# Attention over paged values: probabilities and values as unsplit fp32 in two column halves of TensorE, in place of a high and a low part on the whole array

## The reference, cut to what matters

```python
def mla_attend(q_lat, q_rope, ckv, krope, mask):
    s = (jnp.einsum('bthr,bsr->bhts', q_lat, ckv)
         + jnp.einsum('bthe,bse->bhts', q_rope, krope)).astype(jnp.float32)
    s = jnp.where(mask[None, None], s, -jnp.inf)
    p = jax.nn.softmax(s, axis=-1).astype(ckv.dtype)
    return jnp.einsum('bhts,bsr->bthr', p, ckv)
```

## Time and profile before

| | |
|---|---|
| time, median of 3 runs | 899.58 us (899.31 to 901.48) |
| the profiled execution, its own time | 901.31 us |
| its span in the profile | 899.5 us |
| granted TensorE clock in it | 0.998 |
| TensorE busy | 886.8 us, 99% |
| VectorE busy | 588.7 us, 65% |
| ScalarE busy | 472.5 us, 53% |

### The profile page before, as it was taken

How to read it: one execution, slowest core, us unless ns; L and a number is a source line. 1 busy time by engine, 2 the same in 40 slices (tenths; PEclk the granted TensorE clock), 3 DMA queues, 4 the chain that set the end, 5 groups by cost and what they waited for, 6 DMA issues and landing times. The chain is left out here.

```text
span 899.5 us, 15487 instructions
## 1 busy us (share of the span) xinstructions
PE 886.8 (99%) x5569; PEld 807.1 (90%) x5569; DVE 588.7 (65%) x984; ACT 472.5 (53%) x776; POOL 78.3 (9%) x79
## 2 busy tenths in 40 slices
PE   8999999999999999999999999999999999999996
PEld 8989999999999999999999999888887788888885
DVE  6535635442267678787878866867657697564767
ACT  6564431121233567657666753577755545353446
POOL 0003002413100000000000000000000011111022
PEclk9999999999999999999999999999999999999999
DMA  9694444232293577877787764332037546997586
GB/s 349 242 331 169 164 144 152 71 113 87 75 353 96 170 239 243 259 241 248 234 249 240 247 239 167 128 113 75 18 146 276 117 134 158 231 248 234 128 155 211
DMA packets 77164, 168.55 MB, mean 187 GB/s; under 512 B 9672, under 2 KB 44041, under 8 KB 75096
## 3 DMA queue, kind: packets, MB, share of 16 engines
q1 hardware_dynamic: 70960, 143.27, 47.1%
q0 software_dynamic: 4608, 16.78, 10.1%
q10 hardware_dynamic: 1520, 7.51, 2.3%
HBM read 156.14 MB, written 11.50 MB: 186 GB/s over the span
## 5 line engine op out<-in xcount | busy, mean ns | idle before, releaser
L67 PE MATMUL z<-x_hi,w_hi 128*128 128x288 f32 x512 | 152.6, 298 | 0.0
L69 PE MATMUL z<-x_hi,w_lo 128*128 128x288 f32 x512 | 150.8, 295 | 0.0
L68 PE MATMUL z<-x_lo,w_hi 128*128 128x288 f32 x512 | 150.8, 294 | 0.0
L184 ACT ACTIVATE w_hi<-w_raw 128x1024 fp32r<-128x1024 f32 (+2 forms) x62 | 64.9, 1046 | 134.7 <-PE z L69 52.5
L191 DVE TENSOR_TENSOR w_lo<-w_raw,w_hi 128x1024 fp32r<-128x1024 f32 (+2 forms) x62 | 77.2, 1247 | 69.8 <-ACT w_hi L184 69.3
L67 PEld LDWEIGHTS z<-x_hi,w_hi 128*128 128x128 f32 x512 | 96.1, 188 | 2.3 <-issue 0.2
L68 PEld LDWEIGHTS z<-x_lo,w_hi 128*128 128x128 f32 x512 | 96.1, 188 | 1.7 <-issue 0.2
L69 PEld LDWEIGHTS z<-x_hi,w_lo 128*128 128x128 f32 x512 | 96.0, 188 | 0.0
L1988 ACT ACTIVATE o_hi<-o_raw 128x1024 fp32r<-128x1024 f32 x50 | 52.9, 1060 | 78.0 <-PE pa_s L2901 33.3
L2214 DVE TENSOR_TENSOR o_lo<-o_raw,o_hi 128x1024 fp32r<-128x1024 f32 x50 | 61.1, 1222 | 42.6 <-ACT o_hi L1988 42.5
L69 PE MATMUL z_acc<-x_hi,w_lo 128*128 128x288 f32 x256 | 75.1, 293 | 0.0
(11 more groups left out here) (529 smaller groups left out, 2425.8 us busy)
## 6 DMA issues: line engine op xcount, KB each, us to landing
w_raw<-in_w_feat SPq DMA_DIRECT2D x56, 512.0 KB, 4.0
k_raw<-in_cache SPq DMA_DIRECT2D x128, 192.0 KB, 3.0
v_raw<-in_cache SPq DMA_DIRECT2D x128, 128.0 KB, 2.6
o_raw<-in_w_out POOLq DMA_DIRECT2D x30, 512.0 KB, 8.3
o_raw<-in_w_out SPq DMA_DIRECT2D x20, 512.0 KB, 8.5
w_raw<-in_w_mem_kv SPq DMA_DIRECT2D x16, 512.0 KB, 3.5
gate_spill<-gate_tmp SPq DMA_DIRECT2D x16, 288.0 KB, 3.2
mix<-gate_spill SPq DMA_DIRECT2D x4, 1152.0 KB, 11.1
```

What stands on the lines that cost most here:

```text
L67: pe.matmul(out, a[0], b[0], start=start, stop=False, skip_group_check=onto)
L68: pe.matmul(out, a[0], b[1], start=False, stop=False, skip_group_check=onto)
L69: return pe.matmul(out, a[1], b[0], start=False, stop=stop, skip_group_check=onto)
L184: act.activation(hi_slot(s, u)[:, lo:w], s.wraw[:, u % RAW, lo:w], ACT.Copy).then_inc(s.w_hi, 1)
```

## The change

The values are used where the DMA put them, in `v_raw`, and the probabilities are copied once, in fp32, to a `probs_t` of half the width. The 64 columns of a page's probabilities are the weights, so only half the columns of the array are used by a matmul. Its output goes to partitions 0 to 63 of `ps_o` for an even page of the quad and to 64 to 127 for an odd one. The copies of the values' high parts on ScalarE and of the low parts on VectorE are gone, and so are the low parts of the probabilities on VectorE. The two halves of `ps_o` are added as before, by the same instructions.

```diff
         vraw = at("v_raw", [P, VRING, 4, KVR])
-        vh = at("v_hi", [P, HRING, 4, KVR], F32R)
+        at.at += HRING * 4 * 4 * KVR
...
-        pt = at("probs_t", [P, NPAGE + 1, 2 * NS], F32R)
+        pt = at("probs_t", [P, NPAGE + 1, NS])
+        at.at += 4 * (NPAGE + 1) * NS
...
-                        act.activation(pt[:, 0:8, 0:NS], p_p[:].rearrange("p (g r) -> p g r", g=8), ACT.Copy).then_inc(pt_hi, 1)
+                        act.activation(pt[:, 0:8, :], p_p[:].rearrange("p (g r) -> p g r", g=8), ACT.Copy).then_inc(pt_hi, 1)
...
-                    m = n - VLAG + 1
-                    if 0 <= m < QUADS:
-                        values_hi(m)
...
-                def values_lo(m):
-                    dve.wait_ge(v_hi, m + 1)
-                    dve.tensor_tensor(vlo[:, m % VRING, :, :], vraw[:, m % VRING, :, :], f32(vh[:, m % HRING, :, :]),
-                                      ALU.subtract).then_inc(v_lo, 1)
...
-                        dve.tensor_tensor(pt[:, 0:8, NS:2 * NS], p_p[:].rearrange("p (g r) -> p g r", g=8),
-                                          f32(pt[:, 0:8, 0:NS]), ALU.subtract).then_inc(pt_lo, 1)
...
                         if m % 4 == 0:
-                            pe.wait_ge(pt_lo, 3 * (m // 4) + 1)
+                            pe.wait_ge(pt_hi, 3 * (m // 4) + 1)
                             if m:
                                 pe.wait_ge(o_sb, m // 4)
                         if m % 4 >= 2:
-                            pe.wait_ge(pt_lo, 3 * (m // 4) + m % 4)
-                        pe.wait_ge(v_lo, m + 1)
+                            pe.wait_ge(pt_hi, 3 * (m // 4) + m % 4)
+                        pe.wait_ge(v_in[m % VRING], 64 * (m // VRING + 1))
                         for j in range(4):
                             g = 4 * (m % 4) + j
-                            pe.matmul(p_o[:, 0:KVR], pt[:, g, :], vh[:, m % HRING, j, :], start=g == 0, stop=False)
-                            last = pe.matmul(p_o[:, 0:KVR], pt[:, g, :], vlo[:, m % VRING, j, :], start=False, stop=False)
+                            last = pe.matmul(p_o[mine(j, 0), 0:KVR], pt[:, g, :], vraw[:, m % VRING, j, :], start=g < 2, stop=False)
                         if m % 4 == 3:
-                            pe.wait_ge(zeros, 3)
-                            pe.matmul(p_o[:, 0:KVR], pt[:, 16, :], vs_hi[:], start=False, stop=False)
-                            last = pe.matmul(p_o[:, 0:KVR], pt[:, 16, :], vs_lo[:], start=False, stop=True)
+                            for i in range(2):
+                                c = slice(P * i, P * i + P)
+                                last = pe.matmul(p_o[mine(i, 0), c], pt[:, 16, :], vs[:, c], start=False, stop=True)
                         last.then_inc(pv, 1)
```

More of the change, by code:

```diff
@@ L808, in middle_stage @@
         ckt_s, krt_s = at("ckt_s", [P, 2 * NS]), at("krt_s", [P, NS])
-        vs_hi, vs_lo = at("vs_hi", [P, KVR], F32R), at("vs_lo", [P, KVR], F32R)
+        at.at += 2 * 4 * KVR
+        vs = s.kvn[:, 4, 0:KVR]
         pages = at("pages", [1, DB * NPAGE], I32)
@@ L828, in middle_stage @@
         klo = place(nc, kr_raw, "k_lo", [P, KRING, 4, KW], F32R)
-        vlo = place(nc, v_raw, "v_lo", [P, VRING, 4, KVR], F32R)
         at = Map(nc, kr_raw + 2 * 4 * 4 * KW)
@@ L868, in middle_stage @@
         rope_ps, roped, qrt_ps, qrt_hi, qrt_lo = sem("q_ropep"), sem("q_roped"), sem("q_qrtp"), sem("q_qrthi"), sem("q_qrtlo")
-        kt_ps, kt_sb, vs_done = sem("q_ktp"), sem("q_kts"), sem("q_vs")
+        kt_ps, kt_sb = sem("q_ktp"), sem("q_kts")
         s.middle_sums = z[:, (2 * FEATS - 1) % 3, 0:TH]
@@ L873, in middle_stage @@
         k_in, v_in = [sem(f"s_kin{i}") for i in range(KRING)], [sem(f"s_vin{i}") for i in range(VRING)]
-        kt_hi, kt_lo, kr_lo, v_hi, v_lo = sem("s_kthi"), sem("s_ktlo"), sem("s_krlo"), sem("s_vhi"), sem("s_vlo")
+        kt_hi, kt_lo, kr_lo = sem("s_kthi"), sem("s_ktlo"), sem("s_krlo")
         sc_ps, sc_low, sc_sb = sem("s_scps"), sem("s_sclow"), sem("s_scsb")
@@ L878, in middle_stage @@
         wqr_in, wqr_done = sem("o_wqrin"), sem("o_wqr")
-        pa_ps, pb_ps, pc_ps, pt_hi, pt_lo = sem("s_paps"), sem("s_pbps"), sem("s_pcps"), sem("s_pthi"), sem("s_ptlo")
+        pa_ps, pb_ps, pc_ps, pt_hi = sem("s_paps"), sem("s_pbps"), sem("s_pcps"), sem("s_pthi")
         pv, o_low, o_sb, ot_ps, ot_sb = sem("s_pv"), sem("s_olow"), sem("s_osb"), sem("s_otps"), sem("s_otsb")
@@ L981, in _ @@
                 pool.memset(krt_s[ROPE:P, :], 0.0).then_inc(zeros, 1)
-                pool.memset(f32(vs_hi[NS:P, :]), 0.0).then_inc(zeros, 1)
-                pool.memset(f32(vs_lo[NS:P, :]), 0.0).then_inc(zeros, 1)
-                pool.wait_ge(zeros, 3)
+                pool.wait_ge(zeros, 1)
                 pool.wait_ge(lat_ps, 1)
@@ L1016, in keys_hi @@
                     act.activation(kth[:, n % 2, :, :].rearrange("p c (j k) -> p j c k", j=4), keys_t(kraw, n), ACT.Copy).then_inc(kt_hi, 1)
[L1018 to L1022, removed]
                 def exps(b, part):
@@ L1033, in _ @@
                 act.activation(sq[:, 3, old], s.zq[:, 3, old], ACT.Square).then_inc(squared, 1)
-                act.activation(vs_hi[0:NS, :], s.kvn[0:NS, 4, 0:KVR], ACT.Copy).then_inc(vs_done, 1)
                 act.wait_ge(chain, 1)
@@ L1089, in _ @@
                         act.wait_ge(pa_ps, b)
-                        act.activation(pt[:, 0:8, 0:NS], p_p[:].rearrange("p (g r) -> p g r", g=8), ACT.Copy).then_inc(pt_hi, 1)
+                        act.activation(pt[:, 0:8, :], p_p[:].rearrange("p (g r) -> p g r", g=8), ACT.Copy).then_inc(pt_hi, 1)
                     if q == 1 and 1 <= b <= DB:
                         act.wait_ge(pb_ps, b)
-                        act.activation(pt[:, 8:16, 0:NS], p_p[:].rearrange("p (g r) -> p g r", g=8), ACT.Copy).then_inc(pt_hi, 1)
+                        act.activation(pt[:, 8:16, :], p_p[:].rearrange("p (g r) -> p g r", g=8), ACT.Copy).then_inc(pt_hi, 1)
                     if q == 2 and 1 <= b <= DB:
@@ L1097, in _ @@
                             act.wait_ge(ot_sb, 2 * (b - 1))
-                        act.activation(pt[:, 16, 0:NS], p_m[:, NS:2 * NS], ACT.Copy).then_inc(pt_hi, 1)
+                        act.activation(pt[:, 16, :], p_m[:, NS:2 * NS], ACT.Copy).then_inc(pt_hi, 1)
                     if n == STEPS - 1:
@@ L1203, in _ @@
                 dve.tensor_copy(qn[:], p_o[:]).then_inc(qn_sb, 1)
-                dve.wait_ge(vs_done, 1)
-                dve.tensor_tensor(vs_lo[0:NS, :], s.kvn[0:NS, 4, 0:KVR], f32(vs_hi[0:NS, :]), ALU.subtract).then_inc(vs_done, 1)
                 dve.wait_ge(rooted, 2)
@@ L1279, in _ @@
                     if q == 1 and 1 <= b <= DB:
-                        dve.wait_ge(pt_hi, 3 * b - 1)
-                        dve.tensor_tensor(pt[:, 8:16, NS:2 * NS], p_p[:].rearrange("p (g r) -> p g r", g=8),
-                                          f32(pt[:, 8:16, 0:NS]), ALU.subtract).then_inc(pt_lo, 1)
                         e = mine(b - 1, 0)
@@ L1292, in _ @@
                         dve.tensor_tensor(s.wqr_lo[:], s.wqr[:], f32(s.wqr_hi[:]), ALU.subtract).then_inc(wqr_done, 1)
-                    m = n_ - VLAG + 1
-                    if 0 <= m < QUADS:
-                        values_lo(m)
                 dve.wait_ge(wqr_done, 2)
@@ L1393, in _ @@
                     if q == 1 and 1 <= b <= DB:
-                        pe.wait_ge(pt_lo, 3 * b - 2)
+                        pe.wait_ge(pt_hi, 3 * b - 2)
                         for g in range(8):
@@ L1400, in _ @@
                             pe.wait_ge(tail_out, 1)
-                            pe.wait_ge(zeros, 4)
+                            pe.wait_ge(zeros, 2)
                         else:
@@ L1427, in _ @@
                         if b >= 2:
-                            pe.wait_ge(pt_lo, 3 * (b - 1))
+                            pe.wait_ge(pt_hi, 3 * (b - 1))
                         for g in range(8):
```

## The result

The changed kernel takes 905.43 us (904.65 to 905.87, 5 runs) against 899.58: a ratio of 1.0052, 95% interval 1.0041 to 1.0063, or 4.7 us more (3.7 to 5.7). The two medians themselves lie 5.85 us apart, so the time alone gives the difference to about 1 us. The profiled execution took 905.43 us with a span of 903.6, where before's had 899.5.

A forecast was written before the change was run, and what follows sets the result against it. The prediction took TensorE, never idle in the changed stage, as the bound. Streaming -2.7, new tokens 0, changes of shape +7.5, other engines and waits 0 gave +4.8 on 899.6, so 904.4 us, range 896.2 to 912.

The forecast's parts named there:

- TensorE bounds the stage: In the changed stage TensorE has no idle time, so every nanosecond of TensorE is a nanosecond of the kernel.
- Other engines 0: Copies and subtractions removed from ScalarE and VectorE gain 0 us: TensorE covers them and their traffic doesn't slow its matmuls.
- New waits 0: TensorE itself waits for the values' DMA in the changed stage, but the data is already there: 0 us.
- Streaming -2.7: Four pages in side-by-side column halves take 0.868 us, 0.083 less than before; 32 bursts give -2.7 us.
- Changes of shape +7.5: Bursts entering and leaving column halves: 0.33 us in quarters 2 and 3, 0.14 in 0 and 1; 7.5 us over eight sequences.
- The 0.14 for a burst beside the transposes: Bursts in quarters 0 and 1, next to row-half transposes, add one change between row and column halves, 0.14 us each.
- The free change of the 64-column transposes: Lower bound at the bursts: behind transposes with 64-column weights the projection goes on without loss, so the cost would be 0.
- The drain rule: The skill's statement that changing the tiling mode drains TensorE, speaking against the change at 32 places; 7.5 us taken by it.
- The sum: Whole kernel: -2.7 + 0 + 7.5 + 0 = +4.8 us, predicting 904.4 us.
- One after the other: Rival: column halves in a burst do not overlap at all; +34.2 us, 933.8 us; chance 0.20.
- free changes: Rival: bursts enter and leave column halves at no cost; -2.7 us, 896.9 us; chance 0.22, nearly free included.
- Strict order: Rival: matmuls start only in program order, so a burst lasts five slots, not four; +11.7 us, 911.3 us; chance 0.13.

The follow-up runs named there:

- the kernel with one half only: Against the changed kernel, all four pages of a burst go to one half of the array, lower for even quads, upper for odd: 932.09 us.
- The run with eight and eight: Against the kernel with four quads per burst and late loads, first eight pages go to the lower half, last eight to the upper: 920.55 us.

## Why the prediction was right, point by point

**TensorE bounds the stage.** Shown: 240.00 of 240.00 us busy before and after, and 47.5 and 31.1 us taken off the other engines changed nothing. I expected some 50 and 34, so both were overestimated by about 3 us, which costs nothing here.

**Other engines 0.** Shown for the values by putting their splits back: 904.93 against 905.43 us, and the stage 259.31 us both times. The 288-column matmuls keep their 133 ns, as forecast: in the trace after, 17 intervals from 435.77 to 438.01 are 2.24 us, 132 ns each.

**New waits 0.** Shown for this kernel by its waits. The condition behind it, that the values are long there, has an edge: with the loads two steps later it cost 8.8 us.

**Streaming -2.7.** The four slots of 0.217 are in the timeline. That halves of the columns run side by side was inferred from halves of the rows, and the kernel with one half only shows it for columns. What it costs to lose the overlap was expected at 27.8 us (the prediction's 25.1 + 2.7) and measured at 26.7, or 27.4 by the stage.

**Changes of shape +7.5.** This was the term with the widest bounds, 0 to 10.6, and the value taken from the row halves was right. Measured in one burst it is 0.35 us against 0.33 (0.34 in the kernel with one half), and over the kernel 7.6 us. The 0.14 for a burst beside the transposes was measured as 0.15 in quarter 1, and it agrees with the 0.64 us of a sequence: less 2 x (0.35 - 0.083) for the two lone bursts, 0.11 is left for the other two, and with their streaming gain back that is 0.14 each. The free change of the 64-column transposes was not the pattern to go by.

**The drain rule.** A way into parts of the array and out again took 0.35 us for columns and 0.33 for rows. The Trainium skill (TensorEngine Tiling (Array Packing), Key Properties) says that a change of tiling mode drains TensorE. The traces agree in that each change costs time; that a drain is what takes it isn't visible in them.

**The sum.** +4.8 forecast, 5.4 in the stage of the one trace, 4.1 between the spans, 4.7 by the ratio, 5.85 between the medians; 904.4 us forecast and 905.43 measured. The terms are confirmed one by one, but how near 4.8 is to 4.7 is luck: these readings differ by more than the error of the sum.

**The rivals.** One after the other and free changes are refuted by the runs above. Strict order is refuted in the form in which it was priced: a record does overtake. The run with eight and eight shows that the overtaking ends after three waiting records. Of the order, the Trainium skill (TensorE: Matmul & The Clock Gate, on packing small matmuls) says that matmuls start strictly as in the program. The traces here disagree across halves of the columns.

## What to carry to other kernels

When TensorE is busy throughout a stage, count its slots and its changes of shape: relieving the other engines was worth nothing here, as long as TensorE waited for none of them and for no transfer. Plain fp32 in two column halves streams no slower than this split form on the whole array (0.87 against 0.95 us for four pages), but each lone way into halves and out again costs 0.35 us here, so put such matmuls in few long bursts, beside others that already use parts of the array. Look in the old trace for an operation that is already addressed in parts: here the price of row parts, 0.33 us, foretold that of column parts, 0.35. That is one case and no rule.

## What the runs showed of the hardware that I had not expected

A matmul for one column half overtakes waiting matmuls of the other half, up to three of them: with four records ahead (one running) both halves start together, with sixteen ahead the second half starts beside the thirteenth. Alternating the halves page by page therefore kept the overlap here, and long blocks of one half lost part of it: 919.1 against 907.7 us of span for the same work, although the latter had 8.8 us of waits for data and the former 0.5. What limits it to three isn't shown.
